# TensorE's overflow loop and 0/1 product in a two-layer encoder with experts: the loop first, the product behind it

## What is computed

```python
for l in range(DEPTH):                      # DEPTH = 2
    h = rmsnorm(x, norm_mix[l])
    z = h @ w_in[l]
    ...
    x = x + mix @ w_out[l]
    h = rmsnorm(x, norm_ffn[l])
    x = x + hierarchical_moe(h, w_group[l], b_group[l], w_er[l], b_er[l], w1[l], w3[l], w2[l])
return rmsnorm(x, norm_final)
```

## Time and profile before

| | |
|---|---|
| median of 3 runs | 1968.23 us (1967.73 to 1970.68) |
| the profiled execution's own time | 1968.86 us |
| its span, first to last instruction | 1967.0 us |
| mean granted TensorE clock | 0.994 of full |
| PE busy | 1922.5 us, 98% of the span |
| DVE busy | 1423.3 us, 72% |
| ACT busy | 1207.3 us, 61% |
| POOL busy | 154.6 us, 8% |

### The profile page before, as it was taken

One profiled execution on the slowest core, in us unless ns is written; L12 is line 12 of the kernel. 1 busy time (PEld: TensorE's weight loads), 2 busy tenths in 40 slices (PEclk: granted clock), 3 DMA queues, 4 the chain that ended last, 5 costly groups with the idle time before them and its releaser, 6 DMA issues.

```text
span 1967.0 us, 27018 instructions
## 1 busy us (share of the span) xinstructions
PE 1922.5 (98%) x9252; PEld 1574.9 (80%) x9252; DVE 1423.3 (72%) x1818; ACT 1207.3 (61%) x1516; POOL 154.6 (8%) x169
## 2 busy tenths in 40 slices
PE   9999999999999999999999999999999999999997
PEld 7977777878888888888789777778788888888886
DVE  5454443678989899889834544445798998998897
ACT  5454443447777777777644554343577777777775
POOL 1000000130110011010000000001200110110000
PEclk9999999999999999999999999999999999999999
DMA  5221184479999999999621211734999999999992
GB/s 176 64 65 43 43 216 135 182 282 389 385 370 369 381 384 366 378 389 371 217 75 51 65 62 57 220 102 179 338 379 385 384 366 379 386 368 369 382 381 106
DMA packets 158792, 503.54 MB, mean 256 GB/s; under 512 B 22411, under 2 KB 38795, under 8 KB 158705
## 3 DMA queue, kind: packets, MB, share of 16 engines
q1 hardware_dynamic: 146192, 459.70, 63.3%
q0 software_dynamic: 12512, 42.69, 7.0%
HBM read 490.18 MB, written 32.79 MB: 266 GB/s over the span
## 4 chain that ended last, share of the span: by engine, by line
PE 93%; DVE 4%; ACT 1%; issue 1%; DMA 0%; DVEq 0%; SPq 0%; ACTq 0%
PE ps L1586 27%; PE ps L1588 26%; PE ps L1587 26%; PE ps L1823 3%; PE ps L1754 2%; PE ps L1759 2%; PE ps L1809 2%; PE ps L1953 1%; DVE wl L1079 1%; PE ps L1914 1%; PE ps L1868 1%; PE ps L1926 1%; PE ps L1633 1%; DVE gb L1345 1%; DVE ml L1134 0%
## 5 line engine op out<-in xcount | busy, mean ns | idle before, releaser
L1079 DVE TENSOR_TENSOR wl<-raw,wh 128x2048 fp32r<-128x2048 f32 (+1 forms) x402 | 908.2, 2278 | 167.1 <-ACT wh L701 164.4
L701 ACT ACTIVATE wh<-raw 128x2048 fp32r<-128x2048 f32 (+1 forms) x406 | 754.1, 1883 | 67.0 <-PE ps L1588 66.5
L1586 PE MATMUL ps<-wh,xgh 128*128 128x512 f32 x1024 | 414.6, 405 | 0.0
L1588 PE MATMUL ps<-wh,xgl 128*128 128x512 f32 x1024 | 403.4, 394 | 0.0
L1587 PE MATMUL ps<-wl,xgh 128*128 128x512 f32 x1024 | 400.9, 392 | 0.0
L1588 PEld LDWEIGHTS ps<-wh,xgl 128*128 128x128 f32 x1024 | 192.6, 188 | 43.7
L1587 PEld LDWEIGHTS ps<-wl,xgh 128*128 128x128 f32 x1024 | 193.3, 189 | 38.3
L1586 PEld LDWEIGHTS ps<-wh,xgh 128*128 128x128 f32 x1024 | 192.6, 188 | 37.7 <-issue 0.2
L1586 PE MATMUL ps<-wh,hth 128*128 128x512 f32 x512 | 200.7, 392 | 2.0 <-DVE htl L1134 2.0
L1588 PE MATMUL ps<-wh,htl 128*128 128x512 f32 x512 | 201.0, 393 | 0.0
L1587 PE MATMUL ps<-wl,hth 128*128 128x512 f32 x512 | 200.4, 391 | 0.0
(11 more groups left out here) (309 smaller groups left out, 2614.1 us busy)
## 6 DMA issues: line engine op xcount, KB each, us to landing
raw<-in_w SPq DMA_DIRECT2D x512, 512.0 KB, 6.1
raw<-in_w SPq DMA_DIRECT2D x128, 1024.0 KB
raw<-in_w_gate SPq DMA_DIRECT2D x16, 1024.0 KB
xslots<-zrow POOLq DMA_DIRECT2D x2, 6240.0 KB, 35.8
raw<-in_w_out SPq DMA_DIRECT2D x8, 1024.0 KB
xg<-xslots POOLq DMA_DIRECT2D x14, 520.0 KB, 7.2
raw<-in_w_in SPq DMA_DIRECT2D x8, 800.0 KB
raw<-in_w_oa SPq DMA_DIRECT2D x4, 1024.0 KB
```

The lines of the kernel that those rows point to most:

```text
L701: return nc.scalar.activation(dst, src, ACT.Copy)
L1079: return V.tensor_tensor(dst, src, hi.bitcast(F32), ALU.subtract)
L1586: MM(dst, lh, rh, start=first, stop=False)
L1588: return MM(dst, ll, rh, start=False, stop=last)
```

## The change

On TensorE alone, and for layer 0 alone (l < L - 1), `y_product` leaves its place ahead of the overflow loop. It is called behind the loop for the last block that there was, and inside the loop's body it moves from the end to the start (for the block before). Its 8 constant matmuls are left out there. In layer 1 everything stays.

```diff
--- before.py
+++ after.py
@@ -1992,7 +1992,7 @@
 
                 def y_product(b):
                     pe.wait_ge(S["selt_done"], b - (NG - 2))
-                    if isinstance(b, int):
+                    if l == L - 1 and isinstance(b, int):
                         stay_awake(8)
                     for t in range(NT):
                         tok = slice(t * P, (t + 1) * P)
@@ -2005,9 +2005,13 @@
                                ).then_inc(S["yp_ps"], 1)
 
                 def y_settled(b):
+                    if l < L - 1:
+                        y_product(b)
                     pe.wait_ge(S["x8_done"], (b - (NG - 2)) * NT + BASE["x8_done"])
 
-                chained_blocks(pe, pe_block, y_settled, y_product)
+                n_blocks = chained_blocks(pe, pe_block, y_settled, y_product if l == L - 1 else None)
+                if l < L - 1:
+                    y_product(n_blocks - 1)
 
 
 # ---- launch: one core; inputs and outputs as the reference has them ----
```

## The result

22 runs each: 1974.88 us with the change (1965.59 to 1979.59), 1968.41 us before (1966.26 to 1970.70). The ratio is 1.0029 with a 95% interval of 1.0020 to 1.0038. The forecast of 1968.2 was 6.7 us too low, and the range to 1971.0 does not hold the result.

A forecast was written before the change was run, and what follows sets the result against it. TensorE was taken as the bound. A 5.53 us loop plus 12.2 us to layer 1 gave 17.73 us instead of 17.78, so 1968.86 became 1968.8; medians lying 0.63 lower gave 1968.2 us, range 1964.6 to 1971.0.

The forecast's parts named there:

- What bounds the kernel: Whole kernel: TensorE, busy 98% of the span with 93% of the wait chain; its idle microseconds count in the total.
- The constants take no time of their own: Layer 0, before the 0/1 product: the 8 constants only fill the wait for `yl`; without constants and loop, at most 0.3 us earlier.
- The product starts at 979.82: Behind the moved loop in layer 0: loop priced at 5.53 us after the experts' last matmul, product previously at 975.98.
- The upper bound of 9.8 us: Moved loop's length at most: 5.5 us plus 4.3 us that followed one load of instructions.
- At full clock 11.1 us from product to layer 1: From the 0/1 product's start to layer 1's first product, 11.1 us if TensorE's clock stays full.
- With the half clock 12.2: Same stretch, 12.2 us: clock falls at 979.30, about six product matmuls run at half, turning at full.
- the rival without the fall: Clock stays full before the 0/1 product, margin 0.5 us: total 1967.1 us; chance 0.15.
- The sum: Experts' last matmul to layer 1's first product: 5.53 + 12.2 = 17.73 us instead of 17.78, a change of -0.05 us.
- The loop gets longer: Moved loop needs one more load of instructions: layer 1's product 4.2 us later, total 1972.4 us; chance 0.08.
- The loop is short there: Moved loop takes ScalarE's 2.3 us because DMA engines are less busy: 4.4 us sooner, total 1963.8 us; chance 0.17.
- The clock stays low throughout: Half clock through 0/1 product and turning: 3.6 us later, total 1971.8 us; chance 0.07.
- The test that I named: Profile signs: 5.5 us gap behind experts, half clock then full in turning, product 5 us, layer 1 at 992.0.

The follow-up runs named there:

- the kernel with 15 increments: Kernel before without layer 0's 8 constants, plus 15 unread semaphore increments among its gate products, restoring the loop's position: 1968.47 us over 11 runs, ratio 1.0002.
- the short execution: Profiled run of the unedited changed kernel, 1969.22 us, gap 5.26 us; runs of this kind: 10 of 34, median 1967.0 us.
- the long one: Second profiled run of the unedited changed kernel, 1978.84 us, gap 12.60 us; runs of this kind: 24 of 34, median 1976.0 us.
- place 7047: Position of the loop's first instruction in TensorE's stream in the changed kernel, against 7095 before; 1974.88 us over 22 runs.
- without the loop: Changed kernel with TensorE's overflow loop left out in layer 0, other engines keeping theirs: 1963.69 us over 9 runs, ratio 0.9970.
- the empty body: Changed kernel with TensorE's layer 0 overflow loop still walked three times but containing no block code: 1963.85 us over 9 runs, ratio 0.9978.
- one branch and 48: Changed kernel with one test skipping TensorE's whole layer 0 loop, plus 48 unread semaphore increments ahead: 1963.04 us over 8 runs, ratio 0.9971.
- a shift of 241: Kernel before, constants and order kept, with 241 unread semaphore increments among layer 0's gate products: 1975.53 us over 5 runs, ratio 1.0035.
- a shift of 15 down: Kernel before with only layer 0's 8 constants left out, loop still behind the product: 1973.86 us over 5 runs, ratio 1.0035.
- 33 increments: Changed kernel with 33 unread semaphore increments among layer 0's gate products, moving the loop to position 7080: 1969.21 us over 11 runs, ratio 1.0007.
- the one with 48 increments and the loop: Changed kernel, loop kept, with 48 unread semaphore increments among layer 0's gate products, moving the loop to position 7095: 1966.70 us over 11 runs, ratio 0.9990.
- place 7095: Position of the loop's first instruction in TensorE's stream in the kernel before: 1968.41 us over 22 runs.
- 7080: Position of the loop's first instruction in the kernel before without constants (1973.86 us) and the changed kernel with 33 increments (1969.21 us).

## Why the prediction was wrong

**What bounds the kernel** was right: TensorE alone, and a microsecond of its gap is one of the total (12.60 against 5.26 us of gap, 1977.0 against 1967.3 of span; most of the other 2.4 us lies in layer 1, at the places where the granted clock differs between executions).

**The constants take no time of their own**: right within what the times can tell, by the kernel with 15 increments, 1968.5 against 1968.7 of its series. But the step counted only time. Leaving them out also moved the loop, by 15 places in the old order, and that alone cost 5 us. In the change itself their leaving and the product's make 48 places together.

**The product starts at 979.82**: 979.58 in the short execution, 986.76 in the long one. This is the step that failed. I took 5.53 us for the loop "since it is the same loop on the same engine". It is the same loop, but its length is not a property of the loop: 4.0 to 5.8 us in the short form and 10.6 to 12.6 in the long one, by where its instructions and those around it fall (shown by the increments) and, at place 7047, by the execution; what in the loading decides it is not shown. The upper bound of 9.8 us, one load more, was also too low.

**At full clock 11.1 us from product to layer 1**: 11.43 without the loop (976.78 to 988.21) and 11.45 with the empty body (975.42 to 986.87). 0.3 us too little, and at the end of the sum: tile 3's `diag` is there 8.55 us after the product's start, where the sum had 8.5, and from it to layer 1 are 2.88 us instead of 2.55.

**With the half clock 12.2**: 12.75 in the short execution. The fall ahead of the product was right, as was the full clock in the turning, but it came earlier than the present gap had suggested: 0.85 over the loop's 5.25 us puts it at 978.0, 3.7 us behind the experts' last matmul, where the prediction had 979.30, 5.0 us behind. The margin of 0.5 us, on which the rival without the fall rested, was 1.6. The half clock lasted 5.2 us into the product, not the 2.9 that the present turning showed, for 12 matmuls instead of six, and it mattered less than that, since VectorE's additions follow the matmuls at half clock closely (one each 0.85 us).

**The sum** would have stood, on the short form: 18.00 us instead of 17.73, with a loop 0.27 us shorter and a half clock 0.55 dearer than forecast, which partly cancel. The short form's median is 1967.0 us, where 1968.2 was forecast. A third of the executions are of that kind.

**The rivals.** "The loop gets longer" was the right one, at 0.08, and had the right cause: the branches fall elsewhere among the pieces in which instructions are loaded, which one load in the present gap had hinted at. It was priced at one more load, 4.2 us, and came to three or four, 7 us. What should have raised its chance was in the rows: a load of instructions in the middle of the gap, and ScalarE's 2.30 us for the same loop with a small body. I used that difference, 3.2 us, only as a way to gain. "The loop is short there" was half right: with the instructions at the right place it takes 4.0 us ahead of the product, which makes the changed kernel 2 us faster than the one before; its reason, the load on the DMA engines, was wrong, as a gap of 10.6 us with nearly idle DMA engines shows. "The clock stays low throughout" did not happen in any trace.

**The test that I named** for the profile of the changed kernel came out right in all points but one (the product took 6.2 us, not 5), in a profiled execution that was not typical. What would have shown the error is the spread of the single times, and I had named no test for that.

## What to carry to other kernels

A loop over a large body on TensorE that does nothing kept it standing for 4.0 to 12.6 us here, and how much depends on where the surrounding instructions lie; one test around the whole loop brought 4.0 us against the kernel before in the moved order (5.6 with the increments, not clearly more) and 2.0 in the old one, with no change in what is computed. Before believing that an edit of a few instructions ahead of such a branch is better or worse, shift the stream without any other change (some increments of an unused semaphore where the engine has time) and time both. And look at all the single times before the one trace: two clusters are two forms, and the trace shows one of them.

## What the runs showed of the hardware

**TensorE's instructions come in pieces, and the way over a large body depends on where they are cut.** q8 carries TensorE's instructions, as the traces let one conclude: one load for about every 25 us while TensorE runs straight on (22 from 21 to 546 us), none in the 355 us in which it repeats the middle blocks' loop, and in all 51 loads without the overflow loop, 53 in the kernel before, 54 in the changed one's short execution and 56 in its long one. The kernel before from 560 to 915 us (no row of instruction loads), and q8's row from 915 to 975 us:

```profile
q1 hardware_dynamic: 34875, 129.37, 97.3%
q0 software_dynamic: 1446, 4.07, 3.0%
```

```profile
q8 instruction: 3, 0.05, 0.3%
```

53 loads make 0.87 MB, 16 KB each. The Trainium skill, "Runtime: NRT & Kernel Launch", section "Instruction fetch mechanics", says the same of the size, a block of 256 instructions, and that a taken branch to code that isn't resident waits for a DMA of it. The trace agrees on the size, and the kernels agree with the block of 256: a shift of 241, which is 15 less than a block, gives the long form (1975.5) just as a shift of 15 down does (1973.9). That the branch waits for the load fits the loads in the gaps; no trace shows the wait itself.

**The loads follow each other slowly even on nearly idle DMA engines.** In the long gap with a DMA share of 0.04 they start at 977.0, 977.5, 980.9 and 984.3, the last three 3.4 us apart, though each takes 1.1 to 2.2 us. The product starts at 984.86, while the last of them is under way (to 985.4).

**Two forms at one place.** In all four profiled executions of the changed order at place 7047, the short ones have two loads within 0.5 us of each other ahead of the experts' last matmul's end (973.2 and 973.6, 972.6 and 972.8), and the long ones have one there (973.3, 973.8) and the next 5.7 and 3.2 us later. The short executions with 33 increments and with one branch and 48 show such a pair too (971.2 and 971.6, 971.3 and 971.6), the one with 48 increments and the loop doesn't. So it looks settled by a small difference at or ahead of the branch. Which one stays open: I found no event in the traces that comes earlier in the one form than in the other, and no kernel was made to force it.

**What a place is good for stays open too.** Sorted by their times, place 7095 was short in each of 126 runs of the kernel before (1966.3 to 1971.7) and in 33 of 33 of three others, and 7080 long in 10 of 10 (one of them a block later) behind the product, but short in 10 of 11 behind the experts' last unit. A rule that says which places are good for which code isn't had from so few places.
